# Query's rotary halves as two tiles, and low weight halves in the free columns of the gates' and the rotary key's tile

## The chip, the cores and the metric

The kernel runs on one core of one Trainium2 chip. The metric is the device time of one execution in microseconds (us), as the median of several runs. Before the change it is 1583.11 us (three runs, 1582.89 to 1584.04).

## The reference, cut to what matters

Two transformer blocks in a row on 512 tokens of width 1024, all in float32. The first has a convolution branch and an mLSTM branch and a gated feed-forward, the second a retention branch, a latent attention (MLA) branch with rotary positions, a feed-forward and an embedding branch. What the change touches:

```python
# first block: eight columns of the input projection are the input and forget gates of four heads
gates = if_pre                      # h @ w_in[:, 6144:6152] + b
# second block: latent attention
qh = (rmsnorm(cq, mla_q_norm) @ w_uq).reshape(B, S, 8, 96)
q  = concatenate([qh[..., :64], rope(qh[..., 64:], positions)])
k_rope = rope(kr[:, :, None, :], positions)          # kr = xn @ w_in[:, 2688:2720], 32 columns

def rope(x, positions):             # half = 16 here
    x1, x2 = x[..., :half], x[..., half:]
    return concatenate([x1 * cos - x2 * sin, x2 * cos + x1 * sin], axis=-1)
```

## The kernel before, in words

**Products.** Activations lie with their features on the 128 partitions and the 512 tokens along the free dimension. To come near float32 precision each weight and each activation is split into a high half (rounded to the fast format fp32r) and a low half (the rest). A product of a 128-column weight tile over 1024 inputs (eight blocks k of 128) is 24 matmuls of 512 columns: high weight on high activation and low weight on high activation for each k (`hl`, L1578 and L1579), then high weight on low activation for each k (`lo`, L1586). They accumulate in one of the PSUM banks.

**Weights.** A load of up to 128x1024 weights is a *unit*. SP loads it into one of four `raw` buffers (L1475), ScalarE writes the high half `sph` (L1754) as soon as the unit three before it has been used up, and VectorE writes the low half `spl` (L2026); for units 6 to 24 a second ScalarE pass and an adding DMA from POOL make the low half instead (`BY_DMA`). There are three `sph` and `spl` buffers.

**Order.** A planner, `plan()`, writes one list of steps, and each engine runs its own part of every step in exactly that order; semaphores are waited on in it. In `gemm` (L220) unit n is multiplied, the split of unit n+2 is put into the list after its first four blocks, and `between()` is called three times: after the first half of `hl`, after the second, and after the evacuation. `between()` first puts in what is due in `later_ops` (operations put off by a tick), then a step of the side generators and then the background work, which in the first block is convolution taps on VectorE (L2075, 3.2 taps per tick around the gates; none during the first query/key tiles).

**The gates.** After the value product (units 16 to 23) comes `w_if`, unit 24: a 128-column tile of which columns 0 to 3 and 32 to 35 are used and the others are zero. Its evacuation `gates` is five activations on ScalarE (L1785 to L1795), the first two from the bank. Then come four query/key tiles (units 25 to 28): ScalarE evacuates one (`qk`, L1803 and L1806), VectorE adds three taps (L2141), ScalarE applies SiLU a tick later. The generator `decays` puts `log_forget` (L2099) behind the first of these, and then four `decay` steps (L2108 to L2116) on VectorE.

**The rotary key.** `w_kr`, unit 159, is a 128-column tile with zeros in columns 0 to 63, the 32 key columns in 64 to 95, and the same with its 16-column halves turned in 96 to 127. VectorE multiplies the one by the cosine, the other by the signed sine, adds, and scales (L2386 to L2396).

**The query.** `w_uq` is four units of two tiles, 384 inputs each (nine matmuls a tile). Tiles 0 and 2 hold the rotary columns of four heads each, tiles 1 and 3 the same turned, tiles 4 to 7 the plain columns. `q_turn` (L2375) multiplies a tile by cosine or sine, `q_rope` (L2380) adds the pair, and SP moves each head's 32 rows into `QH` (L1526, eight transfers). Plain tiles are copied by ScalarE (`q_copy`, L1937). `w_uk` and `w_uv` and then the attention follow.

Of the kernel before, what the change touches and what calls it, by code (L numbers as in the profile page):

```python
# [43 lines left out]

BY_DMA = (*range(6, 25),)

# [79 lines left out]
def plan():  # L126
# [24 lines left out]
    units = []  # L151
# [114 lines left out]
    def gemms(jobs, acts, together=2, hook=None):  # L266
# [694 lines left out]
    def rope_rows(name, dst, b, after):  # L961
        j, free = tmp.take()
        k, free2 = tmp.take()
        add("rope_rows", name, dst, b, after, j, free, k, free2)
        tmp.give(j, ("rope", name, 2))
        tmp.give(k, ("rope", name, 2))
        return [("rope", name, 1)]

# [4 lines left out]

    gemm("w_kr", 0, 8, "n3", kr_evac)

# [30 lines left out]
    def q_evac(i, b, g):  # L1006

        if i >= 4:
            add("q_copy", i - 4, b, g)
            return [("q_copy", 2 * i - 8), ("q_copy", 2 * i - 7)]  # L1010
        j, free = tmp.take()
        add("q_turn", i, b, g, j, free)
        turns[i] = j
        if i % 2:
            add("q_rope", i // 2, turns[i - 1], j)
            tmp.give(j, ("q_sum", i // 2))
            tmp.give(turns[i - 1], *[("rope", ("q", 2 * i - 2 + m), 2) for m in range(4)])
        return [("q_turn", i)]

# [3 lines left out]

    for u in range(4):
        for product in small("w_uq", u, 2, 3, "cq", q_evac):
            product()
# [244 lines left out]
def program(nc, A, out, known):  # L1271
    steps, units = plan()
    ctx = ExitStack()
    with ctx:
# [181 lines left out]
        def _(e):  # L1456
# [64 lines left out]

            def q_rope(i, j, k):
                w.wait_ge(at("q_sum", i), *fenced("q"))
                for m in range(4):
                    h = 4 * i + m
                    e.dma_start(QH[64:96, h, :], TMP[j][32 * m:32 * m + 32, :]).then_inc(  # L1526
                        *up(f"d_q{h}", ("rope", ("q", h), 2), by=16))
# [38 lines left out]
        def _(e):  # L1566
# [14 lines left out]
            def lo(b, acts, n, col, ka, kb, last, labels):  # L1581
                low = HALVES[acts][1]
                for k in range(ka, kb):
                    q = slice(col + (k - ka) * 128, col + (k - ka + 1) * 128)
                    w.wait_ge(at("lo", acts, k))
                    m = e.matmul(P_[b][:], sph(n)[:, q], low[:, k, :], start=False, stop=last and k == kb - 1)  # L1586
                if labels:
                    m.then_inc(*up("s_product", *labels))
# [150 lines left out]
            run({"hl": hl, "lo": lo, "whole": whole, "c_rows": c_rows, "tok": tok, "columns": columns, "columns_two": columns_two, "columns_first": columns_first,  # L1739
                 "columns_last": columns_last, "warm": warm, "spread": spread, "decay_cols": decay_cols, "m_rows": m_rows, "score": score,  # L1740
# [5 lines left out]
        def _(e):  # L1746
# [33 lines left out]

            def gates(b, g, j, free, k, free2):
# [3 lines left out]
                e.activation(IR[:], P_[b][0:4, :], ACT.Identity, bias=vec("b_if", 0, slice(0, 4))).then_inc(  # L1785
                    *up("s_if", ("gate", 0)))
                w.wait_ge(*each(free))
                e.activation(z[p, :], P_[b][p, :], ACT.Identity, bias=vec("b_if", 0, p)).then_inc(
                    *up("s_if", ("gate", 1)))
                w.wait_ge(at("gate", 1), *each(free2))  # L1790
# [122 lines left out]
            def rot_sin(z):  # L1913
                sn = TRIG[:, 2 * z + 1, :]
                w.wait_ge(at("rot_clip", z), *fenced("rot"))
                e.activation(sn, TRIG[:, 2 * z, :], ACT.Sin).then_inc(*up("s_trig", ("sin0", z)))
                w.wait_ge(at("sin0", z))
                e.activation(sn, sn, ACT.Copy, scale=const(("sgr", "sgm")[z])).then_inc(*up("s_trig", ("sin", z)))

# [9 lines left out]
            def rv(t, b, g, rcol):  # L1929
                w.wait_ge(at("tile", g), at("rcol"), *fenced("w2"))  # L1930
                e.activation(RV[:, t, :], P_[b][:], ACT.Copy, scale=keep(rcol + t, 1)).then_inc(  # L1931
                    *up("s_rv", ("rv", t)))

            def q_copy(i, b, g):
# [70 lines left out]
            def pg(i, b, g, j, free):  # L2005
# [3 lines left out]

            run({"begin": begin, "split": split, "csil": csil, "square": square, "rsqrt": rsqrt, "glu": glu, "gates": gates, "decay_cols": decay_cols, "qk": qk,  # L2010
                 "qk_silu": qk_silu, "m_rows": m_rows, "score": score, "vals": vals, "head_scale": head_scale, "turn": turn,
# [7 lines left out]
        def _(e):  # L2019
# [3 lines left out]
            def split(n, eng):  # L2023
                if eng == "dve":
                    w.wait_ge(at("wh", n))
# [63 lines left out]
            def v(blk, t, b, g):  # L2089
# [3 lines left out]
                                VB[:, half].rearrange("p (a b) -> p a b", a=2), ALU.add).then_inc(  # L2093
                    *up("s_vtok", ("v", blk, t)))

            def log_forget(j, k):
# [275 lines left out]

            def q_turn(i, b, g, j, free):
                w.wait_ge(at("tile", g), at("sin", 1), at("cos", 1), *each(free))
                e.tensor_tensor(TMP[j][:], P_[b][:], SINM if i % 2 else COSM, ALU.mult).then_inc(  # L2375
                    *up("s_rope", ("q_turn", i)))

            def q_rope(i, j, k):
                w.wait_ge(at("q_turn", 2 * i + 1))
                e.tensor_tensor(TMP[j][:], TMP[j][:], TMP[k][:], ALU.add).then_inc(*up("s_rope", ("q_sum", i)))  # L2380

            def rope_rows(name, dst, b, after, j, free, k, free2):
                to = KR[64:96, :]
                w.wait_ge(*each(after), at("sin", 1), at("cos", 1), *each(free), *each(free2))
                w.wait_ge(*fenced("w2"))
                e.tensor_tensor(TMP[j][64:96, :], P_[b][64:96, :], COSM[64:96, :], ALU.mult).then_inc(  # L2386
                    *up("s_rope", ("rope", name, 0)))
                e.tensor_tensor(TMP[k][64:96, :], P_[b][96:128, :], SINM[96:128, :], ALU.mult).then_inc(
                    *up("s_rope", ("rope", name, 1)))
                w.wait_ge(at("rope", name, 1))  # L2390
                e.tensor_tensor(to, TMP[j][64:96, :], TMP[k][64:96, :], ALU.add).then_inc(
# [127 lines left out]
            def pg(i, b, g, j, free):  # L2519
# [5 lines left out]
            run({"split": split, "sum": total, "rsqrt": rsqrt,  # L2525
                 "sum_pairs": sum_pairs, "mod_dots": mod_dots, "c_copy": c_copy, "ada": ada, "glu_mul": glu_mul, "tap": tap, "conv_sum": conv_sum, "v": v, "log_forget": log_forget, "decay": decay,
                 "decay_rows": decay_rows, "decay_cols": decay_cols, "qk": qk, "m_rows": m_rows, "weigh": weigh,
# [110 lines left out]
def layout(x):  # L2638
# [27 lines left out]
    uq = x["w_uq_2"][0].reshape(384, 8, 96)  # L2666
    plain, turn = uq[:, :, 0:64].reshape(384, 512), uq[:, :, 64:96].reshape(384, 256)
    turned = np.concatenate([uq[:, :, 80:96], uq[:, :, 64:80]], axis=2).reshape(384, 256)
    o["w_uq"] = _several(np.concatenate([turn[:, 0:128], turned[:, 0:128], turn[:, 128:256], turned[:, 128:256], plain],
                                        axis=1), 2)  # L2670
    ukv = x["w_ukv_2"][0].reshape(256, 8, 128)
# [69 lines left out]
```

## Time and profile before

| | before |
|---|---|
| median of 3 runs | 1583.11 us |
| profiled execution: span from first to last instruction | 1580.9 us |
| profiled execution: time of its own | not recorded apart from the span |
| TensorE busy | 1564.6 us, 99% |
| VectorE busy | 972.8 us, 62% |
| ScalarE busy | 666.0 us, 42% |
| GpSimd busy | 103.2 us, 7% |
| matmuls | 7030 |

The span is that of one execution, and the median is of others. Matmuls overlap at their ends, so the distance of their starts tells their pace and not their mean duration.

### The profile page before, as it was taken

What the parts mean: (1) busy time and instruction counts of PE and PEld (TensorE: products, weight loads), DVE (VectorE), ACT (ScalarE), POOL (GpSimd) and SP (SyncE); (2) the same over time, 40 slices, a digit from 0 to 9 for tenths busy, and PEclk for the clock granted to TensorE, in tenths of its full rate; (3) what the DMA queues carried; (4) which work ended last, traced back from release to release, by engine and by line L of the source; (5) the groups of instructions that cost most, each with busy time, mean ns of one, the idle gap of its engine ahead of it and who ended that gap; (6) DMA issues with size and microseconds to landing.
All of it is one profiled execution on the core that took longest, in us unless ns stands there. A gap on an engine that the chain in (4) does not pass through costs nothing.

```text
span 1580.9 us, 18082 instructions
## 1 busy us (share of the span) xinstructions
PE 1564.6 (99%) x7030; PEld 1268.7 (80%) x7030; DVE 972.8 (62%) x1463; ACT 666.0 (42%) x944; POOL 103.2 (7%) x95
## 2 busy tenths in 40 slices
PE   8999999999999999999999999999999999999998
PEld 3788777787888788888888887778888888888877
DVE  7998988887887643333653446766476444442356
ACT  5543588664542522322333225446354332222223
POOL 0111000000000100000021001000201011000000
PEclk9999999999999999999999999999999999999999
DMA  9787222224565343333233323111333333333331
GB/s 370 179 207 189 80 67 67 71 76 128 180 252 193 121 146 120 94 93 102 84 107 101 107 81 107 60 47 41 112 112 103 106 94 94 97 93 100 97 133 67
DMA packets 53903, 184.91 MB, mean 117 GB/s; under 512 B 6197, under 2 KB 8501, under 8 KB 53562
## 3 DMA queue, kind: packets, MB, share of 16 engines
q1 hardware_dynamic: 51080, 173.79, 34.9%
q0 software_dynamic: 2736, 9.96, 3.3%
q8 instruction: 56, 0.92, 0.2%
q14 instruction: 29, 0.24, 0.0%
q10 hardware_dynamic: 2, 0.00, 0.0%
HBM read 169.05 MB, written 4.19 MB: 110 GB/s over the span
## 4 chain that ended last, share of the span: by engine, by line
PE 91%; DVE 5%; ACT 2%; issue 1%; DMA 0%; ACTq 0%; POOL 0%; DVEq 0%; POOLq 0%
PE bank L1578 26%; PE bank L1586 26%; PE bank L1579 26%; PE bank L1594 2%; PE bank L1606 1%; PE bank L1608 1%; PE bank L1607 1%; PE bank L1679 1%; PE bank L1696 1%; DVE convout L2075 1%; DVE tmp L2141 1%; PE bank L1709 1%; DVE spl L2026 1%; PE bank L1652 1%; PE bank L1702 1%
## 5 line engine op out<-in xcount | busy, mean ns | idle before, releaser
L1578 PE MATMUL bank<-HH,sph 128*128 128x512 f32 x1448 | 573.5, 396 | 2.5 <-ACT rv L1931 0.8
L1579 PE MATMUL bank<-HH,spl 128*128 128x512 f32 x1448 | 564.1, 390 | 0.0
L2026 DVE TENSOR_TENSOR spl<-raw,sph 128x1024 fp32r<-128x1024 f32 (+1 forms) x239 | 301.0, 1261 | 291.0 <-ACT sph L1754 290.7
L1586 PE MATMUL bank<-HL,sph 128*128 128x512 f32 x1448 | 373.2, 394 | 0.0
L1754 ACT ACTIVATE sph<-raw 128x1024 fp32r<-128x1024 f32 (+1 forms) x258 | 265.6, 1030 | 183.5 <-PE bank L1586 145.7
L1578 PEld LDWEIGHTS bank<-HH,sph 128*128 128x128 f32 x1448 | 271.9, 188 | 64.8 <-issue 5.3
L1586 PEld LDWEIGHTS bank<-HL,sph 128*128 128x128 f32 x1448 | 270.6, 188 | 59.8 <-issue 3.9
L1579 PEld LDWEIGHTS bank<-HH,spl 128*128 128x128 f32 x1448 | 272.0, 188 | 57.4 <-issue 1.4
L2075 DVE SCALAR_TENSOR_TENSOR convout<-convin,vecs,convout 128x512 f32<-128x512 f32 x240 | 164.9, 744 | 0.0
L1578 PE MATMUL bank<-midh,sph 128*128 128x512 f32 x352 | 136.9, 389 | 0.0
L1579 PE MATMUL bank<-midh,spl 128*128 128x512 f32 x352 | 136.9, 389 | 0.0
L1911 ACT ACTIVATE midh<-tmp 128x512 fp32r<-128x512 f32 x44 | 27.8, 633 | 186.1 <-DVE tmp L2276 97.8
L1586 PE MATMUL bank<-midl,sph 128*128 128x512 f32 x352 | 87.6, 389 | 0.0
L1578 PEld LDWEIGHTS bank<-midh,sph 128*128 128x128 f32 x352 | 66.1, 188 | 13.7
L1586 PEld LDWEIGHTS bank<-midl,sph 128*128 128x128 f32 x352 | 66.1, 188 | 13.7
L1579 PEld LDWEIGHTS bank<-midh,spl 128*128 128x128 f32 x352 | 66.1, 188 | 13.7
L2565 POOL TENSOR_TENSOR tmp<-tmp,tmp 128x512 f32<-128x512 f32 x27 | 35.2, 1315 | 511.5 <-ACT tmp L1769 511.5
L2276 DVE TENSOR_TENSOR tmp<-tmp,bank 128x512 f32<-128x512 f32 x22 | 15.1, 688 | 56.1 <-PE bank L1586 55.3
L2141 DVE SCALAR_TENSOR_TENSOR tmp<-xpad,vecs,tmp 128x512 f32<-128x512 f32 x48 | 36.0, 750 | 13.3 <-ACT tmp L1806 12.1
L2589 POOL TENSOR_TENSOR midl<-tmp,midh 128x512 fp32r<-128x512 f32 x22 | 28.6, 1298 | 231.8 <-ACT midh L1911 231.8
L2046 DVE CUSTOM_DVE_ANT_0 more<-more,crow,vecs 128x1024 f32<-128x1024 f32 x32 | 40.5, 1279 | 3.0 <-DMA more<-in_w_ada 3.0
L1903 ACT ACTIVATE tmp<-bank 128x512 f32<-128x512 f32 x22 | 13.2, 599 | 63.2 <-PE bank L1586 63.2
(303 smaller groups left out, 1623.9 us busy)
## 6 DMA issues: line engine op xcount, KB each, us to landing
raw<-in_w_in SPq DMA_DIRECT2D x69, 512.0 KB, 3.6
raw<-in_w_up SPq DMA_DIRECT2D x66, 512.0 KB, 3.5
more<-in_w_ada SPq DMA_DIRECT2D x32, 512.0 KB, 4.6
raw<-in_w_down SPq DMA_DIRECT2D x32, 512.0 KB, 3.5
raw<-in_w_gate SPq DMA_DIRECT2D x22, 512.0 KB, 3.5
spl<-raw POOLq DMA_DIRECT2D x19, 512.0 KB, 6.1
ada<-in_w_ada SPq DMA_DIRECT2D x16, 512.0 KB, 11.0
raw<-in_w_down SPq DMA_DIRECT2D x16, 384.0 KB, 3.1
```

The costliest lines, as they stand in the source:

```text
L1578: e.matmul(P_[b][:], sph(n)[:, q], hi[:, k, :], start=k == 0, stop=False)
L1579: e.matmul(P_[b][:], spl(n)[:, q], hi[:, k, :], start=False, stop=False)
L1586: m = e.matmul(P_[b][:], sph(n)[:, q], low[:, k, :], start=False, stop=last and k == kb - 1)
L1594: m = e.matmul(P_[b][:], raw(n)[:, token(k)], FULL[acts][:, k, :], start=k == 0, stop=k == 7)
L1754: e.activation(sph(n), raw(n), ACT.Copy).then_inc(*up("s_w_high", ("wh", n)))
L1911: e.activation(MH[:, i, :], TMP[j][:], ACT.Copy).then_inc(*up("s_cut_a", ("hi", f"m{which}", i)))
L2026: e.tensor_tensor(spl(n), raw(n), sph(n).bitcast(F32), ALU.subtract).then_inc(*up("s_w_low", ("wl", n)))
L2046: e.tensor_tensor_reduce(buf, buf, CROW[n][:], 1.0, vec("b_ada", et), ALU.mult, ALU.add, MOD[:, et:et + 1]).then_inc(*up("s_ada", label))
L2075: ins = e.scalar_tensor_tensor(CO[:, i, :], src, wt, CO[:, i, :], ALU.mult, ALU.add)
L2141: e.scalar_tensor_tensor(TMP[j][:], XP[:, s, k:k + 512], wt, TMP[j][:], ALU.mult, ALU.add).then_inc(*up("s_qk_conv", ("qk_conv", h, z, k)))
L2565: e.tensor_tensor(TMP[a][:], TMP[a][:], TMP[j][:], ALU.add).then_inc(*up("s_sum_p", ("ss", name, i)))
L2589: e.tensor_tensor(ML[:, i, :], TMP[j][:], MH[:, i, :].bitcast(F32), ALU.subtract).then_inc(*up("s_cut_p", ("lo", "m2", i)))
```

## The change

The gates' and the rotary key's tiles have 64 free columns. After the change the low halves of the weights are written there, into the same stationary tile (`sph`), next to the high halves: one matmul on the high activation then gives both products, in different rows of the bank, and one on the low activation a third (and a fourth, which is not needed but is added too). The tile takes 16 matmuls (`side_by_side`) in place of 24; the two groups of 64 rows are added afterwards, with a copy by ScalarE and an addition by VectorE. For the gates this sum and the five activations behind it are put into `later_ops`, one tick later. Unit 24 leaves `BY_DMA`.

The query's rotary columns are ordered as two tiles, the first 16-column halves of all eight heads and the second halves. Each is multiplied by cosine and by sine, and the results are combined across the tiles. `w_uq` is three units of two tiles; SP moves 16 rows at a time, sixteen transfers, when both sums are there. The sine of the second block is stored without its sign pattern, which the rotary key now applies itself.

```diff
-BY_DMA = (*range(6, 25),)
+BY_DMA = (*range(6, 24),)
...
+    def gemm_halves(src, acts, evac):
+        b, free = main.take()
+        g = new_tile()
+        n = take(src, 0, 0, 1024)
+        for half in range(2):
+            for k0 in (0, 4):
+                add("side_by_side", b, acts, n, half, k0, free, [("unit", n), ("tile", g)] * (half and k0 == 4))
+                if not half:
+                    if k0 == 0:
+                        ready(more=1)
+                    between()
+        done()
+        main.give(b, *evac(b, g))
+        between()
...
-        add("gates", b, g, j, free, k, free2)
+        add("gates_low", b, g, k, free2)
+
+        def log():
+            add("gates_sum", b, j, free, k)
+            add("gates", j, k)
+
+        later_ops.append((tick[0] + 1, log))
         forget.extend((j, k))
-        return [("gate", 0), ("gate", 1)]
+        return [("gate", "sum")]
...
-    gemm("w_if", 0, 8, "n1", gates)
+    gemm_halves("w_if", "n1", gates)
...
-    gemm("w_kr", 0, 8, "n3", kr_evac)
+    gemm_halves("w_kr", "n3", kr_evac)
...
+        k, free2 = tmp.take()
+        add("q_turn", i, b, g, j, free, k, free2)
+        turns[i] = (j, k)
+        if i == 1:
+            (a_cos, a_sin), (b_cos, b_sin) = turns[0], turns[1]
+            add("q_rope", a_cos, a_sin, b_cos, b_sin)
...
-    for u in range(4):
+    for u in range(3):
         for product in small("w_uq", u, 2, 3, "cq", q_evac):
...
+            def q_rope(a_cos, a_sin, b_cos, b_sin):          # SP
+                w.wait_ge(at("q_sum", 0), at("q_sum", 1), *fenced("q"))
+                for h in range(8):
+                    e.dma_start(QH[64:80, h, :], TMP[a_cos][16 * h:16 * h + 16, :])...
+                    e.dma_start(QH[80:96, h, :], TMP[a_sin][16 * h:16 * h + 16, :])...
...
+            def side_by_side(b, acts, n, half, k0, free, labels):          # TensorE
+                if half == 0 and k0 == 0:
+                    w.wait_ge(*each(free))
+                w.wait_ge(at("wl", n))
+                for k in range(k0, k0 + 4):
+                    w.wait_ge(at(("hi", "lo")[half], acts, k))
+                    m = e.matmul(P_[b][:], sph(n)[:, token(k)], HALVES[acts][half][:, k, :],
+                                 start=half == 0 and k == 0, stop=half == 1 and k == 7)
...
+            def gates_low(b, g, k, free2):          # ScalarE
+                w.wait_ge(at("tile", g), *each(free2))
+                e.activation(TMP[k][0:64, :], P_[b][64:128, :], ACT.Copy)...
+
+            def gates(j, k):
                 p = slice(32, 36)
                 z, y = TMP[j], TMP[k]
-                w.wait_ge(at("tile", g), *fenced("v"))
-                e.activation(IR[:], P_[b][0:4, :], ACT.Identity, bias=vec("b_if", 0, slice(0, 4)))...
+                w.wait_ge(at("gate", "sum"), *fenced("v"))
+                e.activation(IR[:], z[0:4, :], ACT.Identity, bias=vec("b_if", 0, slice(0, 4)))...
...
+            def rope_rows(name, dst, b, after, j, free, k, free2):          # ScalarE
+                w.wait_ge(*each(after), *each(free2))
+                e.activation(TMP[k][64:128, :], P_[b][0:64, :], ACT.Copy)...
...
             def split(n, eng):          # VectorE
+                if units[n][0] in ("w_if", "w_kr"):
+                    w.wait_ge(at("wh", n))
+                    ...
+                    e.tensor_tensor(high[:, :, low, :], given[:, :, 1 - low, :],
+                                    high[:, :, 1 - low, :].bitcast(F32), ALU.subtract)...
...
+            def gates_sum(b, j, free, k):          # VectorE
+                w.wait_ge(at("gate", "low"), *each(free))
+                e.tensor_tensor(TMP[j][0:64, :], P_[b][0:64, :], TMP[k][0:64, :], ALU.add)...
...
+                e.tensor_tensor(TMP[j][:], P_[b][:], COSM, ALU.mult)...          # q_turn, VectorE
+                e.tensor_tensor(TMP[k][:], P_[b][:], SINM, ALU.mult)...
...
+                e.tensor_tensor(TMP[a_cos][:], TMP[a_cos][:], TMP[b_sin][:], ALU.subtract)...          # q_rope
+                e.tensor_tensor(TMP[a_sin][:], TMP[a_sin][:], TMP[b_cos][:], ALU.add)...
...
+                e.tensor_tensor(TMP[j][64:128, :], P_[b][64:128, :], TMP[k][64:128, :], ALU.add)...   # rope_rows
+                e.tensor_tensor(TMP[j][64:96, :], TMP[j][64:96, :], COSM[64:96, :], ALU.mult)...
+                e.scalar_tensor_tensor(TMP[k][64:96, :], TMP[j][96:128, :], const("sgm")[96:128], SINM[96:128, :],
+                                       ALU.mult, ALU.mult)...
```

## Rows read from the trace of the kernel before

**Rows 1.** The page: busy time by engine, and granted clock in 40 slices.
```profile
PE 1564.6 (99%) x7030; PEld 1268.7 (80%) x7030; DVE 972.8 (62%) x1463; ACT 666.0 (42%) x944; POOL 103.2 (7%) x95
...
PEclk9999999999999999999999999999999999999999
```

**Rows 2.** TensorE's waits between 150 and 200 us: total, times, longest.
```profile
PE bank L1578 <- DVE spl L2026: 0.6, 1, 0.6
```

**Rows 3.** Timeline of TensorE around the gates: start, duration, instruction, idle before.
```profile
153.87 0.39 PE L1578 MATMUL bank<-HH,sph 128*128 128x512 f32 x1
...
157.50 1.98 PE L1586 MATMUL bank<-HL,sph 128*128 128x512 f32 x8
159.31 0.39 PE L1578 MATMUL bank<-HH,sph 128*128 128x512 f32 x1
...
175.63 0.39 PE L1578 MATMUL bank<-HH,sph 128*128 128x512 f32 x1
...
181.79 0.47 PE L1578 MATMUL bank<-HH,sph 128*128 128x512 f32 x1 [0.56 <-DVE spl L2026]
```

**Rows 4.** Timeline of ScalarE behind the gates' tile.
```profile
159.51 0.68 ACT L1785 ACTIVATE row<-bank,vecs 4x512 f32<-4x512 f32 x1 [4.32 <-PE bank L1586]
...
165.48 1.06 ACT L1754 ACTIVATE sph<-raw 128x1024 fp32r<-128x1024 f32 x1
166.57 0.69 ACT L1803 ACTIVATE xpad<-bank,vecs 128x512 f32<-128x512 f32 x1
```

**Rows 5.** Timeline of VectorE in the same stretch.
```profile
154.07 2.48 DVE L2092 TENSOR_TENSOR vtok<-bank,vbias 128x512 f32<-128x512 f32 x4 [1.07 <-PE bank L1608]
...
160.26 6.04 DVE L2075 SCALAR_TENSOR_TENSOR convout<-convin,vecs,convout 128x512 f32<-128x512 f32 x9
166.57 1.23 DVE L2026 TENSOR_TENSOR spl<-raw,sph 128x1024 fp32r<-128x1024 f32 x1 [0.27 <-ACT sph L1754]
168.14 2.33 DVE L2141 SCALAR_TENSOR_TENSOR tmp<-xpad,vecs,tmp 128x512 f32<-128x512 f32 x3 [0.34 <-ACT tmp L1806]
...
172.95 1.21 DVE L2026 TENSOR_TENSOR spl<-raw,sph 128x1024 fp32r<-128x1024 f32 x1
...
180.44 1.21 DVE L2026 TENSOR_TENSOR spl<-raw,sph 128x1024 fp32r<-128x1024 f32 x1
```

**Rows 6.** Timeline of TensorE: starts of rotary key, next tile, query and `w_uk`.
```profile
935.31 0.39 PE L1578 MATMUL bank<-HH,sph 128*128 128x512 f32 x1
...
940.75 0.39 PE L1578 MATMUL bank<-HH,sph 128*128 128x512 f32 x1
...
956.03 0.48 PE L1578 MATMUL bank<-cqh,sph 128*128 128x512 f32 x1
...
972.49 0.39 PE L1578 MATMUL bank<-kvh,sph 128*128 128x512 f32 x1
```

**Rows 7.** Timelines of VectorE and ScalarE: low half 162, and two 64x512 operations.
```profile
943.83 0.96 DVE L2026 TENSOR_TENSOR spl<-raw,sph 128x768 fp32r<-128x768 f32 x1
...
955.68 0.69 DVE L2401 TENSOR_TENSOR tmp<-bank,trig 64x512 f32<-64x512 f32 x1
...
974.08 0.59 ACT L1942 ACTIVATE kh<-bank 64x512 f32<-64x512 f32 x1
```

**Rows 8.** Stretches near the end: busy by engine, granted clock, DMA share, GB/s.
```profile
1528.00:1529.00 1.00, 1.00 (x5) 0.85 (x4) 1.00 (x2) 0.00 (x0) 0.00 (x0) 0.50 0.68 279
...
1530.00:1531.00 1.00, 1.00 (x2) 0.34 (x1) 0.97 (x3) 0.62 (x1) 0.00 (x0) 0.50 1.07 459
1531.00:1532.00 1.00, 1.00 (x5) 0.61 (x4) 1.00 (x2) 0.31 (x2) 0.00 (x0) 0.99 0.92 393
```

**Rows 9.** Query's transfers, their landing, the split behind them, landing of loads.
```profile
962.75 2.50 SPq L1526 DMA_DIRECT2D qh<-tmp  x4
...
DMA to landing us min/median/max: 2.0/3.0/4.2
...
985.96 1.08 ACT L1754 ACTIVATE sph<-raw 128x1024 fp32r<-128x1024 f32 x1
...
raw<-in_w_in SPq DMA_DIRECT2D x69, 512.0 KB, 3.6
```

More of the change, by code:

```diff
@@ L966, in rope_rows @@
         tmp.give(k, ("rope", name, 2))
-        return [("rope", name, 1)]
+        return [("rope", name, "sum")]
     def kr_evac(b, g):
@@ L1006, in q_evac @@
     def q_evac(i, b, g):
-        if i >= 4:
-            add("q_copy", i - 4, b, g)
-            return [("q_copy", 2 * i - 8), ("q_copy", 2 * i - 7)]
+        if i >= 2:
+            add("q_copy", i - 2, b, g)
+            return [("q_copy", 2 * i - 4), ("q_copy", 2 * i - 3)]
         j, free = tmp.take()
[L1012 to L1018, printed above, removed]
+        k, free2 = tmp.take()
[4 more added lines that the diff above has]
+            add("q_rope", a_cos, a_sin, b_cos, b_sin)
+            tmp.give(b_cos, ("q_sum", 1))
+            tmp.give(b_sin, ("q_sum", 0))
+            tmp.give(a_cos, *[("rope", ("q", h), 2) for h in range(8)])
+            tmp.give(a_sin, *[("rope", ("q", h), 2) for h in range(8)])
+        return [("q_turn", i, 1)]
     def k_evac(i, b, g):
@@ L1520, in w2_begin @@
                     e.dma_start(RD[:, h, :], A["ret_decay"][:, h, :]).then_inc(*up(f"d_rd{h}", ("rd", h), by=16))
[L1522 to L1526, printed above, removed]
+            def q_rope(a_cos, a_sin, b_cos, b_sin):
+                w.wait_ge(at("q_sum", 0), at("q_sum", 1), *fenced("q"))
+                for h in range(8):
+                    e.dma_start(QH[64:80, h, :], TMP[a_cos][16 * h:16 * h + 16, :]).then_inc(
+                        *up(f"d_q{h}", ("rope", ("q", h), 0), by=16))
+                    e.dma_start(QH[80:96, h, :], TMP[a_sin][16 * h:16 * h + 16, :]).then_inc(
                         *up(f"d_q{h}", ("rope", ("q", h), 2), by=16))
@@ L1737, in mix_mla @@
                 m.then_inc(*up("s_turned", ("mo_tr", i)))
-            run({"hl": hl, "lo": lo, "whole": whole, "c_rows": c_rows, "tok": tok, "columns": columns, "columns_two": columns_two, "columns_first": columns_first,
+            run({"hl": hl, "lo": lo, "side_by_side": side_by_side, "whole": whole, "c_rows": c_rows, "tok": tok, "columns": columns, "columns_two": columns_two, "columns_first": columns_first,
                  "columns_last": columns_last, "warm": warm, "spread": spread, "decay_cols": decay_cols, "m_rows": m_rows, "score": score,
@@ L1779, in glu @@
                     *up("s_gate", ("glu_gate", i)))
-            def gates(b, g, j, free, k, free2):
+            def gates_low(b, g, k, free2):
+                w.wait_ge(at("tile", g), *each(free2))
+                e.activation(TMP[k][0:64, :], P_[b][64:128, :], ACT.Copy).then_inc(*up("s_if", ("gate", "low")))
+            def gates(j, k):
                 p = slice(32, 36)
                 z, y = TMP[j], TMP[k]
-                w.wait_ge(at("tile", g), *fenced("v"))
-                e.activation(IR[:], P_[b][0:4, :], ACT.Identity, bias=vec("b_if", 0, slice(0, 4))).then_inc(
+                w.wait_ge(at("gate", "sum"), *fenced("v"))
+                e.activation(IR[:], z[0:4, :], ACT.Identity, bias=vec("b_if", 0, slice(0, 4))).then_inc(
                     *up("s_if", ("gate", 0)))
-                w.wait_ge(*each(free))
-                e.activation(z[p, :], P_[b][p, :], ACT.Identity, bias=vec("b_if", 0, p)).then_inc(
+                e.activation(z[p, :], z[p, :], ACT.Identity, bias=vec("b_if", 0, p)).then_inc(
                     *up("s_if", ("gate", 1)))
-                w.wait_ge(at("gate", 1), *each(free2))
+                w.wait_ge(at("gate", 1))
                 e.activation(y[p, :], z[p, :], ACT.Abs).then_inc(*up("s_if", ("gate", 2)))
@@ L1915, in rot_sin @@
                 w.wait_ge(at("rot_clip", z), *fenced("rot"))
+                if z == 1:
+                    e.activation(sn, TRIG[:, 2 * z, :], ACT.Sin).then_inc(*up("s_trig", ("sin", z)))
+                    return
                 e.activation(sn, TRIG[:, 2 * z, :], ACT.Sin).then_inc(*up("s_trig", ("sin0", z)))
                 w.wait_ge(at("sin0", z))
-                e.activation(sn, sn, ACT.Copy, scale=const(("sgr", "sgm")[z])).then_inc(*up("s_trig", ("sin", z)))
+                e.activation(sn, sn, ACT.Copy, scale=const("sgr")).then_inc(*up("s_trig", ("sin", z)))
             def rot_cos2(z):
@@ L1932, in rv @@
                     *up("s_rv", ("rv", t)))
+            def rope_rows(name, dst, b, after, j, free, k, free2):
+                w.wait_ge(*each(after), *each(free2))
+                e.activation(TMP[k][64:128, :], P_[b][0:64, :], ACT.Copy).then_inc(*up("s_qkv", ("kr_low",)))
             def q_copy(i, b, g):
@@ L2008, in pg @@
                     *up("s_gate", ("pg_gate", i)))
-            run({"begin": begin, "split": split, "csil": csil, "square": square, "rsqrt": rsqrt, "glu": glu, "gates": gates, "decay_cols": decay_cols, "qk": qk,
+            run({"begin": begin, "split": split, "csil": csil, "square": square, "rsqrt": rsqrt, "glu": glu, "gates": gates, "gates_low": gates_low, "rope_rows": rope_rows, "decay_cols": decay_cols, "qk": qk,
                  "qk_silu": qk_silu, "m_rows": m_rows, "score": score, "vals": vals, "head_scale": head_scale, "turn": turn,
@@ L2023, in split @@
             def split(n, eng):
-                if eng == "dve":
+                if units[n][0] in ("w_if", "w_kr"):
+                    w.wait_ge(at("wh", n))
+                    high = sph(n).rearrange("p (k two c) -> p k two c", two=2, c=64)
+                    given = raw(n).rearrange("p (k two c) -> p k two c", two=2, c=64)
+                    lo = units[n][0] == "w_if"
+                    low = 1 if units[n][0] == "w_if" else 0
+                    e.tensor_tensor(high[:, :, low, :], given[:, :, 1 - low, :],
+                                    high[:, :, 1 - low, :].bitcast(F32), ALU.subtract).then_inc(
+                        *up("s_w_low", ("wl", n)))
+                elif eng == "dve":
                     w.wait_ge(at("wh", n))
@@ L2094, in v @@
                     *up("s_vtok", ("v", blk, t)))
+            def gates_sum(b, j, free, k):
+                w.wait_ge(at("gate", "low"), *each(free))
+                e.tensor_tensor(TMP[j][0:64, :], P_[b][0:64, :], TMP[k][0:64, :], ALU.add).then_inc(
+                    *up("s_decay", ("gate", "sum")))
             def log_forget(j, k):
@@ L2371, in latent, with q_turn @@
                     *up("s_latent", ("latent", name, i)))
[L2373 to L2380, printed above, removed]
+            def q_turn(i, b, g, j, free, k, free2):
+                w.wait_ge(at("tile", g), at("sin", 1), at("cos", 1), *each(free), *each(free2))
+                e.tensor_tensor(TMP[j][:], P_[b][:], COSM, ALU.mult).then_inc(*up("s_rope", ("q_turn", i, 0)))
+                e.tensor_tensor(TMP[k][:], P_[b][:], SINM, ALU.mult).then_inc(*up("s_rope", ("q_turn", i, 1)))
@@ L2382, in rope_rows, with q_rope @@
+            def q_rope(a_cos, a_sin, b_cos, b_sin):
+                w.wait_ge(at("q_turn", 0, 1), at("q_turn", 1, 1))
+                e.tensor_tensor(TMP[a_cos][:], TMP[a_cos][:], TMP[b_sin][:], ALU.subtract).then_inc(
+                    *up("s_rope", ("q_sum", 0)))
+                e.tensor_tensor(TMP[a_sin][:], TMP[a_sin][:], TMP[b_cos][:], ALU.add).then_inc(
+                    *up("s_rope", ("q_sum", 1)))
             def rope_rows(name, dst, b, after, j, free, k, free2):
                 to = KR[64:96, :]
-                w.wait_ge(*each(after), at("sin", 1), at("cos", 1), *each(free), *each(free2))
+                w.wait_ge(at("kr_low"), at("sin", 1), at("cos", 1), *each(free))
@@ L2666, in layout @@
     uq = x["w_uq_2"][0].reshape(384, 8, 96)
[L2667 to L2670, printed above, removed]
+    plain = uq[:, :, 0:64].reshape(384, 512)
+    first, second = uq[:, :, 64:80].reshape(384, 128), uq[:, :, 80:96].reshape(384, 128)
+    o["w_uq"] = _several(np.concatenate([first, second, plain], axis=1), 2)
     ukv = x["w_ukv_2"][0].reshape(256, 8, 128)
```

14 lines of the change are left out of this document (9 added, 5 removed).

## Prediction

> **What bounds the kernel now.** I read the page first: TensorE is busy 99% of the span, and its granted clock reads 9 in all forty slices, so the end of the kernel is the end of its instruction stream [rows 1]. The list of TensorE's waits comes next. In the stretch around the gate projection it holds one entry, 0.6 us, on VectorE's low weight halves [rows 2]. A kernel like this gains what is taken out of TensorE's stream and loses what makes that stream wait; nothing else moves its end. I then read the timelines of the two places that the diff touches. In the first, TensorE's own timeline gives the pace: a tile of 24 matmuls takes 5.44 us, so one takes 0.2267 us, and unit 24 (the gates) runs from 153.87 to 159.31 [rows 3]. ScalarE's timeline has the chain of gate activations right behind it, and ScalarE goes on only when that is done [rows 4]. VectorE's timeline shows what the page hides: from 160.26 to 181 it hardly rests, and it hands unit 29 its low half later than TensorE wants it (the 0.6 us) [rows 5]. So at this place VectorE's order decides.
>
> **Matmuls taken away.** The gate tile and the rotary key tile go from 24 to 16 matmuls each, the query from 8 tiles of 9 to 6 of 9: 8 + 8 + 18 = 34. At 0.2267 us each that is 1.81 + 1.81 + 4.08 = 7.71 us, if TensorE is the bound at all three places. The pace at the other two is the same: 24 in 5.44 us for the key tile, 72 in 16.46 us for the query [rows 6].
>
> The Trainium skill ("TensorE: Matmul & The Clock Gate", section "Wait — 56ns, not 53.3ns?") gives 215.7 ns start to start for 512 columns at the full clock; by it the 34 would be worth 7.33 us. The rows' 226.7 ns is what I use.
>
> **Gates: what is moved.** Before, the chain of five activations reads the bank and starts when the tile ends: 159.51 to 165.48, 5.97 us with two table loads [rows 4]. After, ScalarE copies 64 rows out (0.6 us, as its 64x512 copy [rows 7]), VectorE adds the halves, and only then does the chain start. Both are put off by one tick: they stand behind the split of unit 27, on both queues. In plan order VectorE has: low half 26, nine taps, low half 27, the new sum, the taps of the first query/key tile, the first decay, low half 28. The nine taps run 160.26 to 166.30 [rows 5], and they start no sooner than now: VectorE waits at 154.07 for the last value tile, whose end the change doesn't move. (Its one new op before that, unit 24's low half on 512 columns in place of a DMA, costs some 0.7 us like the 64x512 op of [rows 7], and goes into the 1.07 us that VectorE idles there [rows 5].)
>
> Step by step: low half 27 starts at 166.30 (ScalarE has its high half ready: TensorE is done with unit 24 at 157.50, the copy ends at 158.3, the high half at 159.4). It takes 1.13 to the next start, so the sum starts at 167.43 and takes 0.69 [rows 7], end 168.12. The chain on ScalarE then runs 168.16 to 174.13. Behind it on ScalarE stands the evacuation of unit 25, and VectorE's taps on that tile start 1.57 us later, as they do now (166.57 to 168.14, [rows 4, 5]): at 175.70 in place of 168.14. VectorE, which is full here, stands for 7.6 us on it, with everything behind in its queue. Low half 28 moves from 172.95 to 180.51, low half 29 from 180.44 to 188.00: 7.56 us each.
>
> TensorE meanwhile arrives 1.81 us early: unit 28 would start at 173.82 instead of 175.63, and waits until 180.51 + 1.21 + 0.14 (the 0.14 as before unit 29 now, 181.65 to 181.79 [rows 3, 5]) = 181.86, a gap of 8.0 us. It runs 5.44 us and waits at unit 29 until 188.00 + 1.35 = 189.35. That start is 181.79 now. Behind it both engines go on as they did, 7.56 us later: the order of work is fixed and no engine can use the gap. Net at the gates: **+7.56 us**, the 1.81 us saved included.
>
> Bounds: if the sum came as early as it could (at 158.3, with VectorE idle), the chain would end at 165 and cost nothing; but even then low half 29 is bound by VectorE at 181.65, plus 0.69 for the sum, and less the 0.27 and 0.34 us waits that go [rows 5]: the 1.81 us would not be had either, the place is worth 0. I take +7.56, since VectorE's queue is a fixed order. Upwards: the gap and the clock, below.
>
> **The clock.** Where TensorE did only narrow matmuls for some us near the end, the granted clock was 0.50 (1.2 GHz) from 1528 to 1531 and 0.99 (2.4 GHz) in the microsecond behind it [rows 8]: 3 us at half speed. After an 8 us gap I expect the same in unit 28: 3 us at half speed delay it by 1.5 us. Unit 28 has 2.05 us to spare before low half 29 (187.30 to 189.35), so it costs 0 to the sum. The Trainium skill (same page, section "What's actually happening") says that the default state is throttled and activity releases it; it is a rule against a change that opens a gap, and the rows agree with it.
>
> **Rotary key.** Unit 159 runs 935.31 to 940.75 [rows 6] and ends at 938.94 after. The halves are added with one more copy on ScalarE (0.6) and one more op on VectorE (0.69): VectorE works from 939.8 through five ops of 0.7 to 943.4, where it is now done at 943.83 [rows 7]. Low half 162, next, isn't needed before the query tiles. What follows on VectorE hangs on tiles 160 and 161, which come 1.81 us earlier. **-1.81 us**; bounds 0 and -1.81, and I take the latter, since no matmul waits for the key's ops and VectorE ends them 0.4 us sooner than now.
>
> **Query.** Two tiles with two products each in place of four with one: four products and two sums, as before. Banks: the first is read until about 960.5 in times of before, the second until 962.9, and their next tiles (the third and fourth of plain columns) want them at 964.3 and 966.4. The plain tiles' copies on ScalarE pass one by one. **-4.08 us**; bounds +1 (below) and -4.08.
>
> SP: eight transfers become sixteen. Four issues take 2.50 us now [rows 9], so sixteen take 10.0 us in one block, some 964.3 to 974.3 in times of before. Behind them stands the load of the unit that ScalarE splits at 985.96 now [rows 9] and at 981.9 after. Issued at 974.3 and with 3.6 us to land [rows 9], it is there at 978, 4 us early. The pieces themselves land 2.0 to 4.2 us after issue [rows 9], by 978.5; the first score reads head 0 alone, landed by 969. If an issue took twice as long, the load would come 6 us late: a loss up to 6; I take 0.
>
> Hidden: one sign multiplication less on ScalarE in the middle stage, one POOL transfer less, one load, high half and low half less for the query. None is on a path; 0.
>
> **Sum.** +7.56 - 1.81 - 4.08 = **+1.67 us**. The profiled execution's span is 1580.9; its total isn't recorded, the median of the three runs is 1583.11, 2.2 above the span. 1583.1 + 1.7 = **1584.8**. A measurement here can tell 0.2%, 3.2 us, so this is "no change" (1579.9 to 1586.3), by two large terms that cancel.
>
> **Rivals.** (1) No delay at the gates: VectorE reaches the sum early enough for the chain to lie beside its taps. Then the place is worth 0 and the rest -5.89: 1577.2. For it: before, ScalarE's chain was hidden beside those taps. Against: nine taps stand ahead of the sum in the same queue. 0.15. (2) All three places pay: -7.71, 1575.4. Against it is the VectorE-bound unit 29. 0.05. (3) Slower: TensorE after the gap stays at 1.2 GHz for the whole of unit 28. 24 matmuls at 0.4533 take 10.88 us, 5.44 more, less the 2.05 us to spare: +3.4, 1588.2. It decides from the tenth slow matmul on (2.05 / 0.2267 = 9); the rows show 3 us, seven of that length. By the skill's rule of activity a dense unit 28 releases the clock, which bears against it. 0.15. The forecast has 0.65.
>
> The range that holds the time 8 times in 10 is 1577.0 to 1588.5, down to rival 1 and up to rival 3. Faster by over 0.2%: rivals 1 and 2, 0.20. Slower by over 0.2%: rival 3 and 0.08 of the forecast (a slower sum, a later load), 0.23. Within: 0.57.
>
> **What would show it.** TensorE with a wait of about 8 us on VectorE's low half, some 20 us behind the gates, and one up to 2 us behind it; the new sum on VectorE at about 167.4 and the first gate activation at 168.2; VectorE idle 7.6 us behind the sum, until 175.7; the granted clock at half in unit 28; the key tile 3.6 us long, the query's tiles 12.2 us, with no new wait up to the first scores. If the sum stands at 160 or the wait is under 3 us, the first step is wrong, and the time is under 1580.

## The result, and the profile after

| | before | after |
|---|---|---|
| median | 1583.13 us (20 runs, 1581.85 to 1585.55) | 1585.34 us (20 runs, 1583.67 to 1587.42) |
| ratio | | 1.0013 (95%: 1.0008 to 1.0019) |
| span of the profiled execution | 1580.9 us | 1583.6 us |
| matmuls | 7030 | 6996 |

34 matmuls fewer, and 2.2 us slower by the medians (1.3 to 3.0 by the interval), below the 0.2% named ahead. The page's first line now has TensorE at 98% and its busy time 6.6 us shorter than in [rows 1]; the slices of its row show one 7 where 9 stood, the fifth:

```profile
PE 1558.0 (98%) x6996; PEld 1262.3 (80%) x6996; DVE 972.9 (61%) x1465; ACT 664.6 (42%) x943; POOL 102.2 (6%) x94
...
PE   8999799999999999999999999999999999999998
```

The list of TensorE's waits over the whole span (line, waited for, total, times, longest) points at the place. Before, this entry stood at 0.6 us, once, in the stretch around the gates [rows 2]:

```profile
PE bank L1605 <- DVE spl L2083: 8.0, 2, 7.9
```

TensorE's timeline at the gates (start, duration, instruction, idle before), to be read against [rows 3]. L1623 is the new product, L1605 the old one's `hl`. The gates' tile is 3.63 us long. Unit 28 would have followed at 174.74 and starts at 182.76, unit 29 at 190.24:

```profile
154.79 1.98 PE L1623 MATMUL bank<-HH,sph 128*128 128x512 f32 x8
156.61 1.98 PE L1623 MATMUL bank<-HL,sph 128*128 128x512 f32 x8
158.42 0.39 PE L1605 MATMUL bank<-HH,sph 128*128 128x512 f32 x1
...
182.76 0.77 PE L1605 MATMUL bank<-HH,sph 128*128 128x512 f32 x1 [7.86 <-DVE spl L2083]
183.33 0.63 PE L1606 MATMUL bank<-HH,spl 128*128 128x512 f32 x1
...
188.10 1.98 PE L1613 MATMUL bank<-HL,sph 128*128 128x512 f32 x8
190.24 0.47 PE L1605 MATMUL bank<-HH,sph 128*128 128x512 f32 x1 [0.16 <-DVE spl L2083]
```

VectorE's timeline of the same stretch, against [rows 5]. It shows nine taps, low half 27, the new sum (L2155, 64x512), and then nothing for 7.65 us until ScalarE has evacuated unit 25:

```profile
161.18 6.05 DVE L2132 SCALAR_TENSOR_TENSOR convout<-convin,vecs,convout 128x512 f32<-128x512 f32 x9
167.14 1.23 DVE L2083 TENSOR_TENSOR spl<-raw,sph 128x1024 fp32r<-128x1024 f32 x1
168.27 0.68 DVE L2155 TENSOR_TENSOR tmp<-bank,tmp 64x512 f32<-64x512 f32 x1
176.60 2.33 DVE L2203 SCALAR_TENSOR_TENSOR tmp<-xpad,vecs,tmp 128x512 f32<-128x512 f32 x3 [7.65 <-ACT tmp L1847]
...
181.41 1.21 DVE L2083 TENSOR_TENSOR spl<-raw,sph 128x1024 fp32r<-128x1024 f32 x1
...
188.89 1.21 DVE L2083 TENSOR_TENSOR spl<-raw,sph 128x1024 fp32r<-128x1024 f32 x1
```

ScalarE's, against [rows 4]: high half 27 is written long before, then ScalarE stands 8.8 us for the sum, and the chain runs from 168.99 to 175.04:

```profile
159.12 1.05 ACT L1792 ACTIVATE sph<-raw 128x1024 fp32r<-128x1024 f32 x1
168.99 0.72 ACT L1827 ACTIVATE row<-tmp,vecs 4x512 f32<-4x512 f32 x1 [8.82 <-DVE tmp L2155]
...
175.04 0.69 ACT L1844 ACTIVATE xpad<-bank,vecs 128x512 f32<-128x512 f32 x1
```

TensorE's timeline at the key and the query, against [rows 6]. Key tile 944.16 to 947.79, 3.63 us; query 963.07 to 975.43, 12.36 us in place of 16.46:

```profile
944.16 1.98 PE L1623 MATMUL bank<-HH,sph 128*128 128x512 f32 x8
945.97 1.98 PE L1623 MATMUL bank<-HL,sph 128*128 128x512 f32 x8
947.79 0.39 PE L1605 MATMUL bank<-HH,sph 128*128 128x512 f32 x1
...
963.07 0.47 PE L1605 MATMUL bank<-cqh,sph 128*128 128x512 f32 x1
...
975.43 0.39 PE L1605 MATMUL bank<-kvh,sph 128*128 128x512 f32 x1
```

The account of the 2.7 us between the two spans, from starts in the two timelines: up to the gates +0.92; from unit 24 to unit 29 it takes 35.45 us in place of 27.92, +7.53; from there to the first query matmul -1.41 (772.83 against 774.24); the query -4.10; the rest -0.24. I don't lay the 0.92 on the change: over the kernels below the start of unit 24 lies anywhere from 153.2 to 156.0 us, with the same code ahead of it in most. Most of that spread is a wait of TensorE for a low half that a DMA adds, at about 122 us: none in the earliest kernel (153.23), 0.3 us before, 0.8 us after, 1.9 us in the latest (155.98). So where an experiment speaks of one place, I read the distance from unit 24 to unit 29, which repeats within 0.02 us, and not the span.

### The profile page after: what moved, and what is told of

It is laid out like the page before. It is cut to its first block, busy times and chain, and to the rows that moved or that the text cites. A ratio compares the mean times of both kernels' runs of the same rounds, so it can differ in the third digit from the quotient of the medians.

```text
span 1583.6 us, 18021 instructions
## 1 busy us (share of the span) xinstructions
PE 1558.0 (98%) x6996; PEld 1262.3 (80%) x6996; DVE 972.9 (61%) x1465; ACT 664.6 (42%) x943; POOL 102.2 (6%) x94
## 4 chain that ended last, share of the span: by engine, by line
PE 90%; DVE 6%; ACT 2%; issue 1%; DMA 1%; ACTq 0%; POOL 0%; DVEq 0%; POOLq 0%
PE bank L1605 26%; PE bank L1613 26%; PE bank L1606 26%; PE bank L1632 2%; DVE convout L2132 2%; PE bank L1644 1%; PE bank L1646 1%; PE bank L1645 1%; PE bank L1717 1%; PE bank L1734 1%; DVE tmp L2203 1%; PE bank L1747 1%; DVE spl L2083 1%; DMA spl<-raw 1%; PE bank L1740 1%
## 5 line engine op out<-in xcount | busy, mean ns | idle before, releaser
L1605 PE MATMUL bank<-HH,sph 128*128 128x512 f32 x1432 | 568.5, 397 | 11.3 <-DVE spl L2083 8.0
L1613 PE MATMUL bank<-HL,sph 128*128 128x512 f32 x1432 | 369.3, 394 | 0.0
L1605 PEld LDWEIGHTS bank<-HH,sph 128*128 128x128 f32 x1432 | 269.6, 188 | 74.6 <-issue 16.1
L1605 PE MATMUL bank<-midh,sph 128*128 128x512 f32 x352 | 136.9, 389 | 0.0
L1605 PEld LDWEIGHTS bank<-midh,sph 128*128 128x128 f32 x352 | 66.1, 188 | 13.7
```

What stands on the lines that cost most here:

```text
L1605: e.matmul(P_[b][:], sph(n)[:, q], hi[:, k, :], start=k == 0, stop=False)
```

## The experiments

Theory: the sum of the gates' halves stands behind nine taps and low half 27 in VectorE's fixed queue; the activations wait for it, the evacuation of unit 25 for them, VectorE for that evacuation, and TensorE for VectorE's low halves. Main rival: the gates pay, and the loss is at the query or the key. Further rivals: the half clock after the gap, and the length of the chain rather than its place in the queue.

**Parts alone.** First, the gates undone (the 24 matmuls, activations from the bank, unit 24's low half by DMA):

```diff
-        add("gates_low", b, g, k, free2)
-        ...later_ops.append((tick[0] + 1, log))
+        add("gates_old", b, g, j, free, k, free2)
-    gemm_halves("w_if", "n1", gates)
+    gemm("w_if", 0, 8, "n1", gates)
```

> The gates as before (24 matmuls, activations straight from the bank, unit 24's low half by DMA); rotary key and query as after. Theory (the sum of the gates' halves stands behind nine taps in VectorE's queue, and the activations, the next evacuation and all of VectorE's chain wait for it, +7.6 us, while key and query pay in full): before - 1.81 - 4.08 = 1577.2 us, span about 1575.0, TensorE waits 0.6 us for the low half of unit 29 as before. Rival (the gates' matmuls are saved, and the loss lies at the query: its sixteen transfers, the key's longer chain): after + 1.8 = 1587.1 us.

> e1_gates_undone once more, to stand beside the next on one chip. Theory: 1583.1 - 5.9 = 1577.2 us (1576.1 measured so far).

Measured 1576.10 us (5 runs), ratio to before 0.9956 (0.9942 to 0.9969), and in the second go 1577.69 us (5 runs), 0.9957 (0.9943 to 0.9970). Unit 24 to 29 takes 27.90 and 27.91 us. The rival would have had 1587. TensorE's waits between 150 and 260 us are those of before:

```profile
PE bank L1599 <- DVE spl L2093: 0.5, 1, 0.5
PE bank L1711 <- DVE sc L2228: 0.3, 1, 0.3
```

The gates' part alone, in the kernel before:

```diff
-    gemm("w_if", 0, 8, "n1", gates)
+    gemm_halves("w_if", "n1", gates)
```

> The change at the gates alone; rotary key and query as before. Theory: before + 7.6 = 1590.7 us; from the start of unit 24 to the start of unit 29 it takes 35.5 us (27.92 before). Rival: before - 1.8 = 1581.3 us, 26.1 us from unit 24 to 29.

Measured 1590.99 us, ratio 1.0047 (1.0034 to 1.0059). Unit 24 to 29: 35.46 us (153.53 to 188.99), and the wait of 7.9 us is there with nothing changed at the query or the key:

```profile
PE bank L1600 <- DVE spl L2069: 7.9, 1, 7.9
```

The query's part alone:

```diff
-    gemm_halves("w_kr", "n3", kr_evac)
+    gemm("w_kr", 0, 8, "n3", kr_evac)
```
(on top of the first experiment, with the key's old two products and sum)

> The query's part alone: gates and rotary key with 24 matmuls each as before (the key still applies its sign itself). Theory: before - 4.1 = 1579.0 us, from the first query matmul to the first of w_uk 12.3 us (16.46 before), no new wait up to the scores. Rival (the sixteen transfers take back a part): above 1580.

Measured 1578.23 us, ratio 0.9969 (0.9956 to 0.9981); the query's stretch takes 12.34 us (958.05 to 970.39). The interval, -7.0 to -3.0 us, holds the -4.1; it is too wide to price the key's 1.8 us against the first experiment. The timelines do: from unit 29 to the first query matmul it takes 774.16 us here (183.89 to 958.05), and 772.39 and 772.37 us in the two goes with the key's part in, so the key is worth -1.8 us.

**Is TensorE the bound at the gates at all?** The 16 matmuls stay, the activations read the bank as before, and the low weights' product is left out of the gates:

```diff
-        add("gates_low", b, g, k, free2)
-        ...later_ops.append((tick[0] + 1, log))
+        add("gates_old", b, g, j, free, k, free2)
```

> As after, but the gates' activations read the bank straight at the end of their tile of 16 matmuls, as before; the product of the low weight halves is left out of the gates. Theory: no delay, but the stretch is bound by VectorE, which gains only the 0.27 and 0.34 us it waits there now: unit 24 to unit 29 takes 27.2 us (27.92 before), with a wait of 1.8 us before unit 29, and the time is 1583.1 - 5.9 - 0.7 = 1576.5 us. Rival (TensorE's stream is the bound here too, all 34 matmuls pay): 26.1 us from unit 24 to 29 and 1575.4 us.

Measured 1576.76 us, ratio 0.9956 (0.9944 to 0.9969). The median can't tell 1576.5 from 1575.4, but the timeline can: unit 24 to 29 takes 27.13 us (153.23 to 180.36), with the saved time turned into a wait:

```profile
180.36 0.47 PE L1599 MATMUL bank<-HH,sph 128*128 128x512 f32 x1 [1.58 <-DVE spl L2093]
```

So even free of its sum, the gates' tile pays 0.8 us of its 1.81: VectorE's low halves are the bound there, as they nearly were before. VectorE still writes unit 24's low half here, so that added operation isn't what costs 7.5 us.

**The place in the queue.** Three kernels move the sum forward step by step. In the first, no taps are issued during the gates' tile (`rate` is 1 step and 0 taps a tick), and the nine go to the query/key tiles of head 2 instead, at 1.8 a tick in place of 1:

```diff
+    rate[:] = [1, 0]
     gemm_halves("w_if", "n1", gates)
-TAPS = [[0, 0, 0, 1], [1, 1, 1, 1], [1, 1, 1, 1], ...
+TAPS = [[0, 0, 0, 1], [1, 1, 1, 1], [1.8, 1.8, 1.8, 1.8], ...
```

> As after, but the nine convolution taps of VectorE during the gates' tile are moved to the tiles of head 2 (1.8 taps a tick there in place of 1). Theory (the place in VectorE's queue is the price): the sum ends at 162.1 instead of 168.1 in times of before, unit 28 waits 2 us instead of 8, unit 24 to unit 29 takes 29.4 us (35.45 after), and the time is 1583.1 + 1.5 - 5.9 = 1578.7 us. Rival (the chain of six steps is too long wherever it stands, the taps don't matter): unit 24 to 29 stays at 35 us, 1585 us.

The sum at the tile's end, with the taps left where they are:

```diff
         add("gates_low", b, g, k, free2)
+        add("gates_sum", b, j, free, k)
         def log():
-            add("gates_sum", b, j, free, k)
             add("gates", j, k)
```

> As after, but VectorE's sum of the gates' halves stands at the end of the tile, ahead of three of the nine taps and of low half 27; the activations stay one tick later. Theory: the sum ends 3.1 us sooner in VectorE's queue (six taps ahead of it, not nine and a low half), the activations, the evacuation and the low halves 28 and 29 each come 3.2 us sooner, unit 24 to unit 29 takes 32.3 us (35.45 after), and the time is 1583.1 + 4.4 - 5.9 = 1581.6 us. Rival (the number of operations ahead of the sum doesn't set it): 35.4 us, 1585.3.

Both of these edits:

> As e6_sum_first, and the nine taps of the gates' tile moved to head 2's tiles. Theory: the sum stands right behind low half 26 and ends at 160.9 in times of before, the activations at 166.9; unit 24 to unit 29 takes 28.3 us (27.92 before), and the time is 1583.1 + 0.35 - 5.9 = 1577.6 us. Rival (moved taps come back as a wait later): above 1579.

| | sum starts after unit 24 (us) | unit 24 to 29, expected | measured | median, expected | measured |
|---|---|---|---|---|---|
| after | 13.48 | - | 35.45 | - | 1585.34 |
| sum first | 10.36 | 32.3 | 32.77 | 1581.6 | 1582.08 |
| taps later | 7.52 | 29.4 | 29.49 | 1578.7 | 1579.34 |
| both | 6.39 | 28.3 | 28.36 | 1577.6 | 1577.54 |

From the top row to the last the sum comes 7.09 us sooner and unit 29 comes 7.09 us sooner. The chain is as long in all four (6.04 to 6.05 us on ScalarE); only its place changed. That settles the rival of the chain's length. VectorE's timeline of the last of them, the sum right behind low half 26:

```profile
160.48 1.22 DVE L2084 TENSOR_TENSOR spl<-raw,sph 128x1024 fp32r<-128x1024 f32 x1
161.62 0.68 DVE L2156 TENSOR_TENSOR tmp<-bank,tmp 64x512 f32<-64x512 f32 x1
162.22 1.21 DVE L2084 TENSOR_TENSOR spl<-raw,sph 128x1024 fp32r<-128x1024 f32 x1
169.94 2.33 DVE L2204 SCALAR_TENSOR_TENSOR tmp<-xpad,vecs,tmp 128x512 f32<-128x512 f32 x3 [6.52 <-ACT tmp L1848]
```

"Sum first" is 0.47 us off the expected distance. There the gap is 4.75 us, the clock falls all the same, and unit 28 (179.37 to 187.28, 7.91 us) ends 0.44 us behind low half 29 (written from 185.49, so usable at about 186.84): I had left the clock out of that sum.

**The clock.** Eight matmuls are put into the gap (the trace has two records for each):

```diff
             rate[:] = [1, TAPS[h][z]]
+            if h == 0 and z == 3:
+                warm(*([512] * 8))
```

> As after, with eight matmuls of 512 columns of the vector tile, some 7.5 us, put into TensorE's gap before unit 28. Theory: the half clock costs unit 28 about 1.6 us and hides in the wait before unit 29, so with the clock kept the wait before unit 29 grows from 0.16 to about 2 us, unit 24 to unit 29 stays at 35.45 us, and the time stays that of after, 1585.3. Rival (the half clock is part of the loss): 1.6 to 3 us less, 1582.5 to 1583.7.

Measured 1586.04 us (11 runs), ratio 1.0017 (1.0008 to 1.0026), against 1.0013 for after. Unit 24 to 29: 35.45 us, to the hundredth. Unit 28 now takes its full-clock time, and what it gained is a wait:

```profile
174.25 7.03 PE L1666 MATMUL bank<-vecs,ones 128*128 128x512 f32 x16
182.27 0.47 PE L1607 MATMUL bank<-HH,sph 128*128 128x512 f32 x1 [0.99 <-DVE spl L2085]
...
189.75 0.47 PE L1607 MATMUL bank<-HH,sph 128*128 128x512 f32 x1 [1.79 <-DVE spl L2085]
```

The half clock cost after nothing.

**Can the gates pay as well?** Two kernels have the sum at the tile's end and also move the four taps behind the value tiles, thirteen in all. They differ in where these go: among the query/key tiles of heads 2 and 3, or behind them.

```diff
+            if (blk, t) == (1, 3):
+                rate[:] = [1, 0]
# heads 2 and 3: 1 -> 1.6 taps a tick        (first kernel)
# gate tiles of heads 0 and 1: 1.6 -> 2.2    (second kernel)
```

> As e6_sum_first, and thirteen taps moved (the four behind the value tiles too), to the tiles of heads 2 and 3 at 1.6 a tick. Theory: the sum is done before ScalarE has written high half 27, so the activations run 159.4 to 165.4 in times of before, VectorE's taps on unit 25 start at 166.9 in place of 168.14, and the low halves 28 and 29 come 1.2 us sooner than before: unit 24 to unit 29 takes 26.7 us (27.92 before), and the time is 1583.1 - 1.2 - 5.9 = 1576.0 us, 1 us below e1_gates_undone. Rival (VectorE pays for the moved taps in heads 2 and 3): not below e1_gates_undone.

> As e8_all_taps_later, but the thirteen taps go behind to the gate tiles of heads 0 and 1 (2.2 a tick in place of 1.6), past the query/key tiles of heads 2 and 3. Theory: unit 24 to unit 29 takes 26.5 us as in e8, and the waits of 1.6 us (SiLU) and 1.0 us that e8 shows later go, since they came from taps among the query/key tiles: 1583.1 - 1.4 - 5.9 = 1575.8 us, 1.4 below e1. Rival (any tap that is moved costs VectorE its time wherever it goes): 1578 to 1579 as e8.

Both take 26.53 us from unit 24 to 29, 1.4 us less than before, as expected (26.7 and 26.5), and lose it again further on. My expectation of the time was wrong for both.

The first: 1578.86 us, with new waits of 1.6 us for a SiLU (at 315.48) and 1.0 us for a low half (at 395.52). The second of these isn't shown to come from the taps: that low half stands, through ScalarE's queue, behind the load of a row vector (`c_row`). ScalarE reads it 5.7 us after its issue here, and 4.1 to 4.8 us after it in the other twelve traces.

The second: 1577.88 us, beside 1577.69 us for the gates undone on the same chip. Its large new wait is at the mean of the layer norm. TensorE's timeline of it and of the kernel with the gates undone, each from the start of the weight tile in which the mean stands:

```profile
368.93 0.39 PE L1607 MATMUL bank<-HH,sph 128*128 128x512 f32 x1
...
372.99 1.12 PE L1730 MATMUL bank<-tmp,ones 128*128 128x512 f32 x2 [2.08 <-DVE tmp L2145]
```
```profile
371.18 0.39 PE L1599 MATMUL bank<-HH,sph 128*128 128x512 f32 x1
...
375.80 1.12 PE L1722 MATMUL bank<-tmp,ones 128*128 128x512 f32 x2 [0.83 <-DVE tmp L2153]
```

The mean stands behind 8 matmuls of its tile in the first and behind 16 in the second. The planner puts the layer norm into the list once no tap is left, and 0.6 more a tick over 24 ticks makes room for 14.4 taps where thirteen were moved, so the taps run out a tick sooner. VectorE's last operation ahead of the mean ends 4.00 us (372.93) and 4.56 us (375.74) behind the start of the tile. So VectorE is 0.56 us earlier there, TensorE asks 8 matmuls, 1.81 us, earlier, and the wait grows by the difference, 1.25 us. That is most of the 1.4 us. In the mean's old place the wait would be 0.3 us, an estimate (2.08 less 1.81) that no kernel tested.

The rival named with it came right in the time, but its reason isn't shown: VectorE isn't full up to the mean. It is busy 164.2 of the 191 us up to there with the gates undone, and 172.2 of 191 us with the taps moved.

By its ratio the best version I ran that computes everything is the change without its gates part, 0.9956 of before (0.9942 to 0.9969). The intervals of the two best with a gates' part (this one, 0.9953 to 0.9978, and "both" in the table, 0.9959 to 0.9981) overlap with it.

## Why the prediction was right, point by point

The profiled execution of after has the gates 0.92 us later than that of before; the expected starts are given with this added.

- **The sum's place and start.** Expected 168.35, seen 168.27. The chain behind it: expected 169.08 to 175.05, seen 168.99 to 175.04 (its first two activations take 0.72 from SBUF where they took 0.68 from the bank). VectorE's taps on unit 25: expected 176.62, seen 176.60.
- **TensorE's two waits.** Unit 28 expected at 182.78, seen 182.76; unit 29 expected at 190.27, seen 190.24. The term is +7.53 where +7.56 was forecast.
- **The clock.** I had taken 3 us at half speed and 1.5 us of delay. The granted clock fell while TensorE still waited: it is 0.66 in the microsecond from 179 and 0.50 from 180 to 186, and the first 3.4 us of unit 28 ran under it. Its first seven matmuls start 0.42 to 0.57 us before the next, and at the pace of its last ones it takes 7.15 us in place of 5.44, 1.7 us of delay. The room left before unit 29 is 0.33 us by that count (the view's 0.16 starts from the last matmul's modelled end), where 0.55 was forecast. The term was mis-sized by 0.2 us inside 2.05 us of room, so the sum is untouched. The rows that I took the 3 us from [rows 8] stand behind narrow matmuls and not behind a gap; that the two come out alike was an assumption. The stretches of after (granted clock is the third number from the end):

```profile
179.00:180.00 1.00, 0.00 (x0) 0.00 (x0) 0.64 (x1) 1.00 (x2) 0.09 (x1) 0.66 0.00 0
180.00:181.00 1.00, 0.00 (x0) 0.00 (x0) 0.86 (x3) 0.97 (x3) 0.00 (x0) 0.50 0.00 0
...
182.00:183.00 1.00, 0.23 (x1) 0.27 (x2) 0.96 (x3) 0.00 (x0) 0.00 (x0) 0.50 0.00 0
...
185.00:186.00 1.00, 1.00 (x4) 0.77 (x3) 0.97 (x3) 0.00 (x0) 0.00 (x0) 0.50 0.57 229
186.00:187.00 1.00, 1.00 (x6) 0.82 (x5) 0.93 (x3) 0.00 (x0) 0.00 (x0) 0.92 0.00 0
```

- **The key.** The tile takes 3.63 us, VectorE is done with it at 952.33 (expected 943.4 + 8.85 = 952.25), and no wait follows. From unit 29 to the query it comes to -1.41 where -1.81 was forecast; in the kernel with the gates undone the same distance gives -1.85 (182.92 to 955.31, against 774.24). The 0.4 us is lost far ahead of the key, at 401.82 us. There a tile waits for VectorE's low half, this for ScalarE's high half, and this, in ScalarE's queue, for the operation that reads the loaded `c_row`:

```profile
398.40 1.06 ACT L1803 ACTIVATE crow<-crow 128x1024 f32<-128x1024 f32 x1 [5.04 <-DMA crow<-in_c_row]
...
400.45 1.23 DVE L2083 TENSOR_TENSOR spl<-raw,sph 128x1024 fp32r<-128x1024 f32 x1 [6.97 <-ACT sph L1792]
```

  The load was issued at 393.63 and read 4.77 us later, against 4.45 us before and 4.26 us with the gates undone. So the term held, and this execution had a late load in it; why it was late isn't shown.
- **The query.** -4.10 for -4.08. The sixteen transfers take SP from 971.09 to 981.16, 10.1 us (10.0 expected), and they land in 2.0 us. The load behind them is issued at 981.26; with 3.6 us to land, the median of its kind, it is there 4 us before its split at 988.90, as worked out.
- **The sum.** +1.67 forecast, +2.2 (1.3 to 3.0) measured. Its large terms, +7.56 and -4.08, were each right to 0.03 us in the profiled execution, so the match isn't luck. Its +2.7 us of span is those terms with the 0.92 ahead of the gates, the late load and -0.24 at the end, which no term of the forecast covers.
- **The bound I gave for a gates' part without delay** (0 for the place) was near: without its sum the place is worth -0.8 (27.13 against 27.92), since ScalarE's and VectorE's small waits go and no 0.69 us is added.
- **Rivals.** "No delay at the gates" was refuted by the 7.9 us wait, "all three pay" is excluded by the no-sum kernel even where the sum costs nothing, and "half clock through unit 28" by seven slow matmuls, fewer than the ten from which it would cost.

## What to carry to other kernels

A kernel that is 99% TensorE is bound by TensorE only on average: before counting matmuls saved, look at the tile for the engine that last hands it something, and walk that engine's queue in its written order from the new operation's place. An operation put off by one tick costs what stands ahead of it in its own engine's queue, not its 0.7 us; here nine taps and a low half made 7.1 of the 7.5 us. And where a planner hangs later steps on the end of some background work, moving that work moves them too: look for where they land, as here the mean of the layer norm, which came eight matmuls sooner and waited 1.25 us longer.

## What the runs showed of the hardware that I had not expected

- After idle gaps of 4.75 us and of 7.9 us alike, TensorE ran at 1.2 GHz afterwards; with the 7.03 us of matmuls in the gap and 0.99 us of idling it did not. Matmuls of 512 columns were then 0.43 us apart in place of 0.227.
- The clock also fell behind a gap of 1.90 us, and only once TensorE was at work again: in "taps later" unit 28 starts at 176.91 at full pace, and the granted clock is 0.91 from 177 to 178 and 0.50 from 178 to 181. With gaps of 0.77 and 1.76 us ("both") it stayed at 1.00. In "taps later" the slow stretch again hid in the wait before unit 29, of which 0.15 us is left.
- SP's issue of a transfer takes 0.59 us whether it moves 32 rows of 2 KB or 16; halving the pieces doubled SP's time, from 4.9 to 10.1 us.
- A VectorE operation on 64 or 4 partitions takes as long as one on 128: 0.68 us for 64x512 (the sum), 0.68 us for 4x512 (L2161), 0.69 us for 128x512 (L2468).
